# Modulation units spread over the gates, a second bank for the turns of memory attention, a rolling down product in layer 1, and most vectors loaded behind the tokens

## What is computed

```python
m_lat = (jax.nn.silu(c) @ w_mod + b_mod)[:, None, :]
m_ctx = jax.nn.silu(c_ctx) @ w_mod + b_mod
...
gates = jax.nn.sigmoid(gate_logits)
merged = gates[..., :D_MODEL] * (branches[0] @ w_branch[0])
for i in range(1, N_BRANCH):
    merged = merged + gates[..., i * D_MODEL:(i + 1) * D_MODEL] * (branches[i] @ w_branch[i])
...
a = jnp.einsum("becd,edf->becf", xs, w_gate)
u = jnp.einsum("becd,edf->becf", xs, w_up)
y = jnp.einsum("becf,efd->becd", jax.nn.silu(a) * u, w_down) * sel_w[..., None].astype(h.dtype)
...
s = jnp.einsum('blhd,bmhd->bhlm', q, k).astype(jnp.float32) * (XA_HEAD_DIM ** -0.5)
p = jax.nn.softmax(s, axis=-1).astype(v.dtype)
o = jnp.einsum('bhlm,bmhd->blhd', p, v).reshape(bsz, seqlen, D_MODEL)
```

## Time and profile before

| | us |
|---|---|
| median of 3 runs (lowest to highest) | 3114.74 (3114.62 to 3118.58) |
| the profiled execution's own time | 3111.43 |
| its span | 3109.6 |
| TensorE busy | 2841.2 (91%) |
| weight loads of TensorE busy | 2025.8 (65%) |
| VectorE busy | 858.0 (28%) |
| ScalarE busy | 347.8 (11%) |
| DMA of 684.05 MB | 220 GB/s in the mean |

### The profile page before, as it was taken

One profiled execution on the slowest core, in us unless ns is written; L12 is line 12 of the kernel. 1 busy time (PEld: TensorE's weight loads), 2 busy tenths in 40 slices (PEclk: granted clock), 3 DMA queues, 4 the chain that ended last, 5 costly groups with the idle time before them and its releaser, 6 DMA issues.

```text
span 3109.6 us, 39609 instructions
## 1 busy us (share of the span) xinstructions
PE 2841.2 (91%) x16504; PEld 2025.8 (65%) x16504; DVE 858.0 (28%) x1787; ACT 347.8 (11%) x710; POOL 52.7 (2%) x92
## 2 busy tenths in 40 slices
PE   7999999998888889999977777899999999998998
PEld 3644444466666667788644343488788887887887
DVE  1322321152222233432311111278622202222201
ACT  0012220020000002121100000011211001011000
POOL 1000000000000001000000000000000000000000
PEclk9999999999999999999998999999999999999999
DMA  8434135149999993233599999933232443342441
GB/s 325 175 143 157 56 157 199 68 157 421 421 420 421 420 411 113 95 107 132 202 415 413 419 418 417 416 140 136 105 122 97 157 144 117 122 142 81 151 148 39
DMA packets 97660, 684.05 MB, mean 220 GB/s; under 512 B 11488, under 2 KB 12640, under 8 KB 16992
## 3 DMA queue, kind: packets, MB, share of 16 engines
q1 hardware_dynamic: 91488, 660.17, 53.7%
q0 software_dynamic: 6016, 21.50, 2.2%
HBM read 678.22 MB, written 3.41 MB: 219 GB/s over the span
## 4 chain that ended last, share of the span: by engine, by line
PE 75%; DMA 19%; DVE 2%; issue 1%; ACT 1%; SPq 1%; ACTq 0%; DVEq 0%
PE ps L605 29%; DMA ring<-units 19%; PE ps L870 11%; PE ps L1032 9%; PE ps L895 3%; PE ps L1337 2%; PE ps L1169 2%; PE ps L623 1%; PE ps L614 1%; PE ps L696 1%; PE ps L692 1%; PE ps L988 1%; PE ps L785 1%; PE ps L916 1%; PE ps L806 1%
## 5 line engine op out<-in xcount | busy, mean ns | idle before, releaser
L1032 PE MATMUL ps<-ring,arena 128*64 128x256 f32 (+1 forms) x4096 | 439.1, 418 | 134.5 <-DMA ring<-units 130.9
L605 PE MATMUL ps<-h,ring 128*128 128x256 f32 (+1 forms) x2176 | 502.6, 393 | 4.9 <-ACT h L1496 4.9
L605 PEld LDWEIGHTS ps<-h,ring 128*128 128x128 f32 x2176 | 413.3, 190 | 92.0 <-issue 37.8
L1032 PEld LDWEIGHTS ps<-ring,arena 128*64 128x64 f32 (+1 forms) x4096 | 287.0, 140 | 274.9 <-issue 187.9
L870 PE MATMUL ps<-u,ring 128*128 128x512 f32 (+1 forms) x1024 | 340.8, 489 | 6.3 <-DMA ring<-units 6.3
L605 PE MATMUL ps<-arena,ring 128*128 128x256 f32 x1408 | 306.6, 379 | 4.7 <-DVE arena L2290 3.4
L605 PEld LDWEIGHTS ps<-arena,ring 128*128 128x128 f32 x1408 | 267.3, 190 | 42.1 <-DVE arena L2290 4.2
L870 PEld LDWEIGHTS ps<-u,ring 128*128 128x128 f32 x1024 | 194.0, 191 | 142.1 <-issue 120.5
L1047 PE MATMUL ps<-ring,arena 128*32 128x256 f32 x2048 | 237.4, 383 | 37.5 <-DMA ring<-units 33.2
L1047 PEld LDWEIGHTS ps<-ring,arena 128*32 128x32 f32 x2048 | 118.0, 109 | 154.5 <-DMA ring<-units 64.7
L2203 DVE COPY u<-ps 32x512 f32<-32x512 f32 (+1 forms) x128 | 70.9, 554 | 245.6 <-PE ps L1032 244.3
(11 more groups left out here) (331 smaller groups left out, 2604.8 us busy)
## 6 DMA issues: line engine op xcount, KB each, us to landing
ring<-units SPq DMA_DIRECT2D x624, 1024.0 KB, 12.5
arena<-quarters POOLq DMA_DIRECT2D x32, 256.0 KB, 2.9
h<-tokens SPq DMA_DIRECT2D x1, 2048.0 KB, 26.0
arena<-neighbours POOLq DMA_DIRECT2D x32, 64.0 KB, 5.7
arena<-tokens POOLq DMA_DIRECT2D x1, 2048.0 KB, 8.9
arena<-memory POOLq DMA_DIRECT2D x2, 1024.0 KB, 5.4
con<-constants SPq DMA_DIRECT2D x1, 1712.0 KB, 20.2
early_values<-arena POOLq DMA_DIRECT2D x6, 256.0 KB, 5.2
```

Source lines behind the costliest of these rows:

```text
L605: last = nc.tensor.matmul(ps[:, g + j, 0:n], w[:, kt, j * P:(j + 1) * P], rhs[:, q * KT + kt, 0:n], start=(q == 0 and kt == 0), stop=(q == ...
L1032: last = nc.tensor.matmul(ps[j * slots:(j + 1) * slots, bank, lo:lo + UC], lhsT[:, kt, 0:slots], w[j][:, kt, :], start=(kt == 0), stop=(kt ...
```

## The change

- **Start**: the first 112 of the 1664 columns of `vec` (condition vectors and modulation bias) are loaded first, the rest behind the tokens. VectorE waits for both before it halves the convolution vectors; that wait stood two instructions further on.
- **Mixing in layer 0**: the stream holds, for each slot, four modulation units, the first gate, four modulation units and the three other gates. TensorE takes the first gate half of chunks c = 0 and 1, then four modulation units (`modulation_rows` into one bank, by `unit_at`), and turns the rows in chunk c = 2. VectorE copies rows in chunks 0 and 1 and adds the bias in chunk 2.
- **Experts in layer 1**: the down product goes through `rolling` as well, on the same bank.
- **Memory attention**: turns alternate between two banks; every mix waits for its own copy; the third turn stands behind the first mix; the mixes' banks are named anew.

```diff
@@ -129,9 +129,11 @@
         for b in range(4):
+            gates = w_in[7 + 4 * ORDER[b]:11 + 4 * ORDER[b]]
             if l == 0:
-                parts.append(w_mod[2 + b])
-            parts.append(w_in[7 + 4 * ORDER[b]:11 + 4 * ORDER[b]])
+                parts += [w_mod[2 + b][:4], gates[:1], w_mod[2 + b][4:], gates[1:]]
+            else:
+                parts.append(gates)
         parts += [units_of(i["w_out"][l]), units_of(i["xa_w_v_2"][l])[1:]]
@@ -468,12 +470,14 @@
         def _(sp):
-            sp.dma_start(vec[:, :], ap["vectors"]).then_inc(vectors_loaded, 16)
+            early = VEC["ln1_g"][0]
+            sp.dma_start(vec[:, 0:early], ap["vectors"][:, 0:early]).then_inc(vectors_loaded, 16)
             sp.dma_start(con[:, 0:P + 2], ap["constants"][:, 0:P + 2]).then_inc(vectors_loaded, 16)
...
             sp.dma_start(h[:, :, :], ap["tokens"]).then_inc(inputs_loaded, 16)
+            sp.dma_start(vec[:, early:], ap["vectors"][:, early:]).then_inc(inputs_loaded, 16)
             for s in range(3):
@@ -558,9 +562,12 @@
-                n = state["unit"]
+                state["unit"] += 1
+                return unit_at(state["unit"] - 1)
+            def unit_at(n):
                 pe_wait_unit(n)
-                state["unit"] += 1
                 return ring[:, n % RING, :].rearrange("p (k c) -> p k c", c=UC)
@@ -832,21 +839,21 @@
-                def modulation_rows(chunk):
+                def modulation_rows(chunk, first):
                     if chunk:
...
                         pe.wait_ge(products_taken, products - 2)
-                    for n in range(2):
-                        w = [unit() for _ in range(4)]
-                        for kt in range(KT):
-                            for q in range(4):
-                                last = nc.tensor.matmul(ps[32 * q:32 * (q + 1), wb + n, 0:UC], cs[:, kt, :], w[q][:, kt, :],
-                                                        start=(kt == 0), stop=(kt == KT - 1))
-                        last.then_inc(units_used, 4)
-                def modulation_columns(n):
-                    pe.wait_ge(rows_kept, n + 1)
+                    w = [unit_at(first + q) for q in range(4)]
+                    for kt in range(KT):
+                        for q in range(4):
+                            last = nc.tensor.matmul(ps[32 * q:32 * (q + 1), wb, 0:UC], cs[:, kt, :], w[q][:, kt, :],
+                                                    start=(kt == 0), stop=(kt == KT - 1))
+                    last.then_inc(units_used, 4)
+                def modulation_columns(chunk, n):
+                    pe.wait_ge(merged_step, chunk)
+                    pe.wait_ge(rows_kept, 2 * n + 2)
                     for t in range(2):
@@ -858,8 +865,9 @@
                     done = 16 * l + chunk
-                    if l == 0 and c == 0:
-                        modulation_rows(chunk)
+                    first = state["unit"]
+                    if l == 0 and c < 2:
+                        state["unit"] += 4
                     w = unit()
@@ -874,8 +882,10 @@
                             if l == 0:
-                                if c == 0:
-                                    modulation_columns(slot)
+                                if c < 2:
+                                    modulation_rows(chunk, first)
+                                if c == 2:
+                                    modulation_columns(chunk, slot)
                                 attend(2 * chunk)
@@ -886,7 +896,9 @@
                         pe.wait_ge(merged_step, done)
-                    if l == 0 and c == 0:
+                    if l == 0 and c < 2:
+                        pe.wait_ge(rows_kept, 2 * slot + c + 1)
+                    if l == 0 and c == 2:
                         pe.wait_ge(columns_kept, slot + 1)
...
@@ -1045,7 +1057,7 @@
                                     last = nc.tensor.matmul(ps[j % 4 * slots:(j % 4 + 1) * slots, banks[j // 4], 0:UC],
-                                                            xcur[:, kt, 0:slots], w[j][:, kt, :],
+                                                            lhsT[:, kt, 0:slots], w[j][:, kt, :],
                                                             start=(kt == 0), stop=(kt == KT - 1))
...
@@ -1072,8 +1084,11 @@
                             pe.wait_ge(act_to_pe, at(act_to_pe, pairs))
-                            for p in range(pairs):
-                                chunks(5, p * UC, hid)
+                            if pairs == 1:
+                                rolling((5,), hid)
+                            else:
+                                for p in range(pairs):
+                                    chunks(5, p * UC, hid)
                             count.skip(y_kept, 1)
...
@@ -1185,19 +1199,16 @@
                     pe.wait_ge(dve_to_pe, at(dve_to_pe))
-                    if c:
-                        pe.wait_ge(act_to_pe, at(act_to_pe))
                     for kb in range(TB):
                         for b in range(TB):
-                            last = nc.tensor.transpose(ps[:, turn_, kb * S + b * P:kb * S + (b + 1) * P],
+                            last = nc.tensor.transpose(ps[:, turn_ + c % 2, kb * S + b * P:kb * S + (b + 1) * P],
                                                        xp[c][:, b, kb * P:(kb + 1) * P], ident)
...
-                mixes = (mix_, score, own[1], own[1] + 1)
+                mixes = (own[1], own[1] + 1, score, score + 1)
                 def mix(c):
-                    if c == 3:
-                        pe.wait_ge(act_to_pe, at(act_to_pe))
+                    pe.wait_ge(act_to_pe, at(act_to_pe))
                     bank = mixes[c]
@@ -1218,10 +1229,10 @@
                 turn(1)
-                turn(2)
                 drained()
...
                 mix(0)
+                turn(2)
                 mix(1)
...
@@ -1663,7 +1674,7 @@
                     act.wait_ge(pe_to_act, at(pe_to_act))
-                    A(xpT[c], ps[:, turn_, :].rearrange("p (a n) -> p a n", n=S), ACT.Copy).then_inc(act_to_pe, 1)
+                    A(xpT[c], ps[:, turn_ + c % 2, :].rearrange("p (a n) -> p a n", n=S), ACT.Copy).then_inc(act_to_pe, 1)
                 state["product"] += 4
@@ -1897,11 +1908,11 @@
             modulation(0)
+            dve.wait_ge(inputs_loaded, 32)
             for name in ("conv_w", "ssm_conv_w", "ssm_conv_b", "conv_ln_g", "conv_ln_b"):
...
             v.memset(beta, 0.0)
-            dve.wait_ge(inputs_loaded, 16)
             v.tensor_scalar(nsink, V("sink"), -1.0, None, ALU.mult)
@@ -2033,12 +2044,11 @@
                         merge(chunk - 1)
-                    if l == 0 and chunk % 4 == 0:
+                    if l == 0 and chunk % 4 < 2:
+                        dve.wait_ge(units_used, at(units_used, 4))
+                        v.tensor_copy(mrow[chunk % 4], ps[:, wb, 0:UC]).then_inc(rows_kept, 1)
+                    if l == 0 and chunk % 4 == 2:
                         n = chunk // 4
-                        dve.wait_ge(units_used, at(units_used, 4))
-                        v.tensor_copy(mrow[0], ps[:, wb, 0:UC])
-                        dve.wait_ge(units_used, at(units_used, 4))
-                        v.tensor_copy(mrow[1], ps[:, wb + 1, 0:UC]).then_inc(rows_kept, 1)
                         dve.wait_ge(rows_turned, n + 1)
```

16 lines of the change are left out of this document (7 added, 9 removed).

## The result

| | before | changed |
|---|---|---|
| median of 4 runs each on one chip, us | 3116.66 (3114.62 to 3122.79) | 3078.12 (3076.58 to 3081.38) |
| ratio of the medians, 95% interval | | 0.9877 (0.9864 to 0.989) |
| profiled execution: own time, span, us | 3111.43, 3109.6 | 3076.58, 3074.8 |
| mean granted clock of TensorE | 0.979 | 0.994 |

The kernel got 38.5 us faster; forecast were 33.6 us and 3081.1 us. Between the two profiled executions the spans differ by 34.8 us. This table takes them apart at points that both time lines of TensorE have. The mixing of layer 0 is counted from the product L752 (L759 in the changed kernel), which stands ahead of chunk 0, and that of layer 1 from its first gate, both to the output product L605 (L612); the last row ends with TensorE's last matmul. "Forecast" is the prediction's term.

A forecast was written before the change was run, and what follows sets the result against it. TensorE held 75% of the span and its waits for weight units 19%, so gains lie where it stands still, clocks low or the stream shortens. 1.2 + 26.5 + 1.7 + 4.2 = 33.6 off 3114.7 gave 3081.1 us, range 3074 to 3091.

The forecast's parts named there:

- The stated ends: Whole kernel: the forecast's own ends, given as 3078 to 3088 us, widened by rivals and clock phases to 3074 to 3091.
- Vectors behind the tokens, 1.2 us: Start: units 0 to 7 come earlier, first token matmul starts at 34.0 to 34.6, not 35.52; 1.2 us gained, ends 0 and 1.9.
- Modulation spread, 26.5 us: Layer 0 mixing: modulation halves behind gate halves remove waits and low clock; 26.5 us gained, ends 19.8 and 27.4.
- The slots: Layer 0 mixing: merge waits and low clock at later slots, and three gate-unit waits, vanish; 16.9 us gained.
- Rivals 1 and 5: Layer 0 mixing: first, units' waits stay, 6.3 us, chance 0.08; other, softmax uncovered, up to 41.0 us, chance 0.03.
- Rival 2: Both attentions and mixing: the low clock stays, 8.4 us more, giving 3089.5 us; chance 0.10.
- Down product rolls, 1.7 us: Layer 1 experts: only the last expert's down product ends sooner, fifteen inner ones gain nothing; 1.7 us gained.
- Rival 3: Layer 1 experts: earlier release shortens the stream, fifteen periods by 0.34 each, 5.1 us more gained, 3076.0; chance 0.07.
- Rival 4: Layer 1's sixteen experts: the roll's matmul time binds, 3.0 us slower each, 48 in all, 3131; chance 0.02.
- Memory attention, 4.2 us: Two attentions: a second bank removes a turn's wait; 3.0 us in one layer, 1.3 in the other; ends 2.5 and 5.9.

The follow-up runs named there:

- second profile: No edit: the kernel before and the changed kernel each profiled once more, one execution each; 3114.41 and 3081.53 us.

## Why the prediction was right, and where its steps failed

- **The total** (3081.1, range 3074 to 3091) holds 3078.12. It is right on the whole because one term, 26.5 of 33.6 us, was right; of the others one came out with the other sign in the changed kernel and two were too small, which partly made up for it; that part of the agreement is luck. The stated ends don't follow from the terms: their low ends are 0, 19.8, 0 and 2.5 us, 22.3 in all, which gives 3092.4 and not 3088, just outside the range of 3091.
- **Vectors behind the tokens, 1.2 us: wrong sign in the changed kernel.** The steps on the transfers hold nearly: the rest of the vectors landed at 32.2 (31.6 to 32.2), unit 8 at 34.65 (33.9 to 34.5). It stands behind the same bytes as before and came 0.7 us later, because the queue starts more thinly: in the first four 1 us slices it moves 0, 30, 122 and 226 GB/s, before 0, 67, 146 and 426, which is 0.26 MB or some 0.6 us at 420 GB/s. The prediction had these 0.6 us for units 0 to 7 and not for unit 8. The failed step is "Nothing waits for units after that until 168 us, so the gain stays": I moved the start of the product and not the length of the pause ahead of it. The pause grew from 2.70 to 4.04 us, and the product behind it took 1.4 us more. The table of the starts shows a pause of 3 us or more and a slow product in six profiles of the seven with this start, and that kernels without the edit differ by as much as the whole term.
- **Modulation spread, 26.5 us: right, step by step.** Chunk 0 was forecast to take 29.3 us and takes 29.3, with a wait of 0.9 (0.97). The slots: 16.9 forecast, 26.35 - (43.0 - 29.3 - 4.05) = 16.7 measured. Rivals 1 and 5 are out: no unit is waited for at any slot, and no chunk but the first waits for a softmax. Rival 2, the low clock that stays, is out in the first profile and came in part in the second, with 1.66 us in the mixing and 1.69 in the first attention, of the 8.4 that it had.
- **Down product rolls, 1.7 us: right place, too small.** At the end of the stage the gain is 1.7 us against the first profile and 2.3 to 2.8 against the others; the failed step is "A queue that never runs dry isn't shortened by an earlier issue. So I cost the fifteen inner experts at nothing". The premise came from a share of 1.01, which doesn't see the thinning. Rival 3 holds in part: the distances shrink, by 1.2 us between the first two profiles and by up to 4.3, not by 5.1. Twelve of the fifteen did come to 29.8 us, and three stayed at 31.3. The whole edit is worth 5.0 us by its own run. I had said that if the experts' period moved at all my reasons were wrong; it moved, by 0.08 us an expert (1.2 / 15), and this reason was. What shortened them is open, as said above.
- **Rival 4**, the roll's matmul time, is out. By the Trainium skill ("TensorE: Matmul & The Clock Gate", "Part 3: Packing small matmuls") column tiles that run together are cheaper than in turn. TensorE's busy time in the 400 us did grow, from 306.6 to 349.6 us, which agrees with the rule; but it lies under the stream, and the distance fell.
- **Memory attention, 4.2 us: right in mechanism, too small.** The term took one layer at full clock and one at low; the profile has both at full: 2.88 + 3.04 = 5.9. With the edit alone the first is low (13.37) and the second isn't. The choice of one each was a coin, which fell the other way in this profile, inside its ends of 2.5 and 5.9; in the second profile it fell as forecast.
- **Outside the terms** the table of the two executions has -1.59, +3.32 and -1.25 us that the edits don't touch. All three are low clock behind pauses that both kernels have: 0.98 and 0.90 us, 1.95 us, and 2.46 us ahead of the second MLP's first product, which takes 110.98 us or 112.2 to 112.4. The second has one value in both second profiles and is chance. The first goes mostly with the mixing's edit, and the short value of the last stands in seven of nine profiles with the attention's edit and in none of five without it; whether the edits shift them is open.

## What to carry to other kernels

Work that waits for nothing belongs between the thing that was just issued and the thing that needs its result: eight half modulations of 3.66 us cost nothing but themselves behind a gate half, and at the head of a chunk they cost 37 us more. Cost a pause by what runs behind it as well, since here pauses of 0.9 to 4.1 us were often followed by a low clock that cost 1.3 to 3.3 us, and others of the same length by none; an edit that only starts the waiting earlier can gain nothing. And where one queue of transfers sets the pace, don't take a full DMA share for a stream that can't get shorter: look at the distance of each turn of the loop, and at GB/s in slices short enough to show one turn.

## What the hardware showed that I had not expected

- A DMA share of 1.01 stood beside 415, 417, 419 and 421 GB/s, and 419 beside distances of 451.50 and of 452.64 us.
- The granted clock is not a function of the kernel alone. In the first attention of the changed kernel the mix behind the same 2.80 us of waiting took 1.96 us in one execution and 2.52 in another, at low clock.
- A low clock came behind a pause as short as 0.90 us (with one of 0.98 just ahead of it) in five profiles of fourteen, and behind one of 1.95 us in thirteen of fourteen, where it cost up to 3.3 us; a pause of 2.84 us was followed by full clock.
- The two opening modulation groups, at 14.3 and 24.3 us, took 4.98 and 5.13 us in one execution of the changed kernel and 5.60 and 5.35 in another; the second token product started at 49.91 and 50.23 us. With the start's edit alone they took 5.98 and 6.13 us, and it started at 48.50.
